# Layer norm shift as one float32r product of a rounded chunk, in a four-sub-layer hybrid decoder trunk on one core

## What is computed

```
def layer_norm(x, g, b):
    xf = x.astype(jnp.float32)
    mu = jnp.mean(xf, -1, keepdims=True)
    var = jnp.mean(jnp.square(xf - mu), -1, keepdims=True)
    return ((xf - mu) * lax.rsqrt(var + LN_EPS) * g + b).astype(x.dtype)

for i in range(DEPTH):                                   # DEPTH = 2, alpha = sqrt 2
    x = layer_norm(DN_ALPHA * x + 0.5 * swiglu(x, ...), ...)            # ln 0, 4
    y = swa_mixer(x, ...) if i == 0 else nsa_mixer(x, ...)
    x = layer_norm(DN_ALPHA * x + y, ...)                               # ln 1, 5
    x = layer_norm(DN_ALPHA * x + mem_cross_attention(x, mem, ...), ...) # ln 2, 6
    x = layer_norm(DN_ALPHA * x + 0.5 * swiglu(x, ...), ...)            # ln 3, 7
```

## Time and profile before

| | |
|---|---|
| Median of 3 runs | 2191.91 us (2190.52 to 2194.28) |
| Profiled execution | 2191.08 us, span 2189.3 us |
| PE busy | 2167.1 us, 99% |
| PEld busy | 1921.7 us, 88% |
| DVE, ACT, POOL busy | 1334.9 us (61%), 1063.5 us (49%), 780.2 us (36%) |
| Chain that ended last | PE 93%, DVE 3%, ACT 1%, POOL 1%, issue 1% |
| Mean granted clock of PE | 0.996 |

### The profile page before, as it was taken

The page is one execution under the profiler, slowest core; times in us unless marked ns, Lnnn a source line. Parts: engine busy times, 40 slices in busy tenths (PEclk is TensorE's granted clock), DMA queues, the critical chain, the costliest instruction groups (busy, mean ns, idle before and its releaser), DMA issues.

```text
span 2189.3 us, 35422 instructions
## 1 busy us (share of the span) xinstructions
PE 2167.1 (99%) x13654; PEld 1921.7 (88%) x13654; DVE 1334.9 (61%) x2315; ACT 1063.5 (49%) x1919; POOL 780.2 (36%) x573
## 2 busy tenths in 40 slices
PE   9999999999999999999999999999999999999998
PEld 8999998878888989898899999887778888989896
DVE  7666666464346938385756666657655346747475
ACT  5435345563445525254643444466654445535353
POOL 3201117557647030305420201555548555120203
PEclk9999999999999999999999999999999999999999
DMA  4333334213313323233232333320004312333332
GB/s 157 116 96 98 106 117 132 78 42 116 117 37 106 108 95 114 90 114 120 85 121 91 101 103 117 115 87 21 21 10 135 106 51 75 116 97 100 103 102 73
DMA packets 58199, 207.50 MB, mean 95 GB/s; under 512 B 6960, under 2 KB 7088, under 8 KB 57264
## 3 DMA queue, kind: packets, MB, share of 16 engines
q1 hardware_dynamic: 56016, 197.68, 29.0%
q10 hardware_dynamic: 2016, 7.55, 0.9%
HBM read 203.10 MB, written 2.10 MB: 94 GB/s over the span
## 4 chain that ended last, share of the span: by engine, by line
PE 93%; DVE 3%; ACT 1%; POOL 1%; issue 1%; DMA 0%; DVEq 0%; ACTq 0%
PE bank L1748 15%; PE bank L1749 14%; PE bank L1750 14%; PE bank L1959 11%; PE bank L1961 11%; PE bank L1960 11%; PE bank L2157 2%; PE bank L2118 2%; PE bank L2090 1%; PE bank L2091 1%; PE bank L1848 1%; PE bank L1849 1%; PE bank L1850 1%; PE bank L1767 1%; PE bank L1778 1%
## 5 line engine op out<-in xcount | busy, mean ns | idle before, releaser
L612 POOL TENSOR_TENSOR w_lo<-w_raw,w_hi 128x1024 fp32r<-128x1024 f32 (+1 forms) x226 | 530.4, 2355 | 1179.2 <-ACT w_hi L789 1179.1
L1748 PE MATMUL bank<-h_hi,w_hi 128*128 128x512 f32 x960 | 381.0, 397 | 2.5 <-DVE h_lo L1552 1.1
L1749 PE MATMUL bank<-h_lo,w_hi 128*128 128x512 f32 x960 | 374.4, 390 | 0.0
L1750 PE MATMUL bank<-h_hi,w_lo 128*128 128x512 f32 x960 | 374.0, 390 | 0.0
L789 ACT ACTIVATE w_hi<-w_raw 128x1024 fp32r<-128x1024 f32 (+1 forms) x227 | 230.5, 1021 | 128.3 <-PE bank L1750 92.4
L1959 PE MATMUL bank<-x_hi,w_hi 128*128 128x256 f32 x864 | 245.2, 284 | 0.3
L1960 PE MATMUL bank<-x_lo,w_hi 128*128 128x256 f32 x864 | 244.5, 283 | 0.0
L1961 PE MATMUL bank<-x_hi,w_lo 128*128 128x256 f32 x864 | 244.5, 283 | 0.0
L1748 PEld LDWEIGHTS bank<-h_hi,w_hi 128*128 128x128 f32 x960 | 180.4, 188 | 47.6 <-issue 4.7
L1750 PEld LDWEIGHTS bank<-h_hi,w_lo 128*128 128x128 f32 x960 | 180.2, 188 | 38.5
L1749 PEld LDWEIGHTS bank<-h_lo,w_hi 128*128 128x128 f32 x960 | 180.5, 188 | 36.1 <-issue 1.9
(11 more groups left out here) (306 smaller groups left out, 5708.1 us busy)
## 6 DMA issues: line engine op xcount, KB each, us to landing
w_raw<-w_dram SPq DMA_DIRECT2D x315, 512.0 KB, 3.5
w_raw<-w_dram SPq DMA_DIRECT2D x64, 448.0 KB, 3.3
f<-mem_dram ACTq DMA_DIRECT2D x5, 1024.0 KB, 6.5
out_dram<-t SPq DMA_DIRECT2D x8, 256.0 KB, 2.2
t<-x_dram SPq DMA_DIRECT2D x2, 512.0 KB, 6.7
f<-cmp_w_dram ACTq DMA_DIRECT2D x1, 1024.0 KB, 5.0
t<-x_dram ACTq DMA_DIRECT2D x2, 256.0 KB, 5.4
t<-x_dram ACTq DMA_DIRECT2D x1, 512.0 KB, 8.0
```

Of the source, the lines that this page charges most:

```text
L612: pool.tensor_tensor(w_lo[:, slot(s), 0:n * P], w_raw[:, s % RAW, 0:n * P], w_hi[:, slot(s), 0:n * P].bitcast(F32), ALU.subtract).then_inc ...
L1748: pe.matmul(dst, w_hi[:, slot(s), w], m_hi[:, k, :], start=k == 0, stop=False)
L1749: pe.matmul(dst, w_hi[:, slot(s), w], m_lo[:, k, :], start=False, stop=False)
L1750: last = pe.matmul(dst, w_lo[:, slot(s), w], m_hi[:, k, :], start=False, stop=k == n - 1)
```

## The change

Four edits:

1. `ones8`, the matrix of 8/1024, becomes float32r. It is still set once by POOL.
2. ACT gets a new instruction in each of the eight sub-layers, `lead_round`: it waits until DVE has added slab 0 to chunk 0 of `t`, and copies that chunk, rounded to float32r, to `lead` (the first part of the tile `pt`). `shift` waits for that copy and multiplies it instead of `t`.
3. `shift` stands behind out slab 2 instead of slab 1 where the sub-layer is no feed-forward (ln 1, 2, 5, 6).
4. `warm(8)` behind the statistics becomes `warm(5)`.

```
-        ones8 = sb("ones8", [P, P])
+        ones8 = sb("ones8", [P, P], F32R)
...
                     for j in range(KC):
                         feed(st.out[part][j] + 3)
+                        if not after and j == 0:
+                            lead_round(st)
...
+            def lead_round(st):
+
+                act.wait_ge(out_free, out_reads(st, len(st.out) - 1, 0))
+                act.activation(lead, t[:, 0, :], ACT.Copy).then_inc(lead_ready, 1)
...
             def out_squares(st, load=None):
                 for j in range(KC):
+                    if j == 0:
+                        lead_round(st)
                     feed(st.out[0][j] + 3)
                     square_chunk(st, j)
...
                 if not st.fill and st is not final:
-                    warm(8)
+                    warm(5)
...
             def shift(st):
                 pe.wait_ge(pool_set, 6)
-                pe.wait_ge(out_free, out_reads(st, len(st.out) - 1, 0))
-                pe.matmul(bank[B_SHIFT][:], ones8[:], t[:, 0, :], start=True, stop=True).then_inc(shift_ready, 1)
+                pe.wait_ge(lead_ready, st.ln + 1)
+                pe.matmul(bank[B_SHIFT][:], ones8[:], lead, start=True, stop=True).then_inc(shift_ready, 1)
...
-                    if j == 1 and part == len(st.out) - 1:
+                    if j == (1 if st.kind == "ffn" else 2) and part == len(st.out) - 1:
                         shift(st)
```

More of the change, by code:

```diff
@@ L365, in build @@
         t4 = [ptf[:, 1024 * i:1024 * i + 1024].rearrange("p (k s) -> p k s", k=4) for i in range(2)]
+        lead = pt[:, 0, :]
         comb = {1: (x_hi[:, 0:4, half[1]], x_lo[:, 0:4, half[1]]), 2: (rows4[0], rows4[1]), 3: (rows4[2], rows4[3]),
@@ L419, in build @@
         out_free = sem("out_free")
+        lead_ready = sem("lead_ready")
         shift_ready = sem("shift_ready")
@@ L616, in _ @@
             pool.memset(ones[:], 1.0 / D).then_inc(pool_set, 1)
-            pool.memset(ones8[:], 8.0 / D).then_inc(pool_set, 1)
+            pool.memset(ones8[:].bitcast(F32), 8.0 / D).then_inc(pool_set, 1)
             pool.memset(one, 1.0).then_inc(pool_set, 1)
```

## The result

| | before | after |
|---|---|---|
| Median | 2191.96 us (2190.52 to 2194.28, 22 runs) | 2195.31 us (2192.86 to 2198.81, 22 runs) |
| Ratio | | 1.0015, 95% interval 1.0009 to 1.0021 |
| Profiled execution | 2191.08 us, span 2189.3 us | 2197.56 us, span 2195.7 us |
| Mean granted clock | 0.996 | 0.993 |

The changed kernel is 3.35 us slower; 2194.8 us were predicted. 0.15% lies under the 0.2% that count as a change here, so it is no change by the stated bound, though the interval says that the small loss is real.

The account below looks back on a forecast made before the run. PE, busy 99% of the span, was taken to bound the kernel. Mixer stops +5.0, cheaper product -3.9, fewer ones -0.3 and clock +2.1 gave +2.9 us, 2194.8 us against the median; range 2190.5 to 2198.5.

Parts of the forecast that it names:

- The bound: Whole kernel: time is what PE's queue takes; an edit elsewhere counts only where it makes PE wait.
- The product: Shift at ln 0, 2, 3, 4, 6, 7: one float32r unit of 0.23 us, saving 0.65 us each, 3.9 together.
- The stops in the mixers: ln 1 and 5: copy ahead of rounding delays slab 3 by 2.5 us each, 5.0 together; PE stands still 3.2 us.
- its cheaper price: POOL's remainder of slab 3 in the mixers: 2.37 us alone, 2.69 beside DVE's sum of two squares.
- Slab 4 in the mixers: ln 1 and 5: two bases (2.54 us) and remainder done at 515.4 to 515.8, wanted at 516.0; no wait.
- a sign that POOL is tighter than it was put: Waits of PE at slab 4 in cross attention or mixers would show this; no size given.
- Fewer ones: ln 6: PE soon waits for POOL's first `x_lo`, so at most 0.35 us saved; 0.3 taken.
- The clock: Behind each mixer stop: falls in about 7 of 10 times, 3.4 us at half rate, 1.4 us each; 2.1 taken.
- the clock takes more: Rival, mixers: two stretches at half rate per stop, up to 3.1 us each, 6.2 together; total +7.0, 2198.9 us; chance 0.17.
- The sum: Whole kernel: +0.8 without the clock and +2.1 for it, +2.9 us, 2194.8 us against the median.
- The parts without the clock: Whole kernel: +5.0 for the mixers, -3.9 for the product, -0.3 for fewer ones, together +0.8 us.
- waits of up to 1.5 us leave no mark on the clock: PE's short waits in the trace, cited for the rival that stops come but the clock stays up: 2192.7 us, chance 0.16.

Follow-up runs that it names:

- the kernel with half the ones: The changed kernel with 6 products of ones instead of 12 in each mixer's stop, between shift and slab 3: median 2193.74 us, ratio 1.0006 of before.
- the kernel that rounds first: The changed kernel with ACT rounding slab 3 ahead of the copy in mixers and cross attention: 2185.05 us against 2191.82 before, ratio 0.9974.

## Why the prediction was right

**The bound.** PE's queue set the time throughout; each edit showed its worth in PE's starts. Right.

**The product.** 0.65 us each at six places. The new shift takes 0.22 us from its start to the next one, and the kernel with the product in the feed-forward alone has a span 2.6 us shorter, 4 x 0.65. In cross attention POOL's remainder was predicted to come with hardly any slack and no wait; that is what the rows show. Right.

**The stops in the mixers.** The path was right: the copy, the rounding behind it, POOL, slab 3. The chain behind DVE's addition was put at 4.16 us and was 4.19 in ln 1 and 4.20 in ln 5 (1654.45 - 1650.25). POOL's remainder took its cheaper price, 2.35 and 2.36 us: it escaped DVE's sum of two squares, which came at 512.39, behind it. So slab 3 is 2.4 us late in each mixer, not the 2.5 I took, and PE stands still for 2.9 us, not 3.2.

**Slab 4 in the mixers.** Here the prediction was wrong, and the falling clock hid it. It had two bases at 2.54 us and slab 4 without a wait, and named a wait there as a sign that POOL is tighter than it was put. But the bases meet the end of one sum on DVE (L1300, until 511.88) and the sum of two squares at 512.39, and take 3.41 us. In the changed kernel PE works slab 3 at half rate behind five of the six stops and needs 6.9 to 8.4 us for it, so POOL is in time. Behind the sixth, where the clock stayed up, slab 4 starts 5.78 us behind slab 3 instead of 5.46. So it does in both mixers with 12 and with 6 products of ones in the stop, and with the copy alone in the kernel before (5.77). That is 0.3 us, and slab 5 comes another 0.1 us late (5.52 to 5.57 us behind slab 4 instead of 5.44). So a mixer costs 2.8 us without the clock, two of them 5.7 against the 5.0 in the sum.

**Fewer ones.** 0.35 us, the bound that POOL's first `x_lo` set; 0.3 was taken. Right.

**The clock.** The mechanism was right and its size too small. I took a fall in 7 of 10 stops and 3.4 us at half rate, 2.1 us in all. Seen were five falls in six, two of them twice as long. Counting only the time at half rate in which PE had work, the three executions of the changed kernel lose 3.0 + 1.5, 1.7 + 3.0 and 1.7 + 0 us, on average 3.6. Each fall spares PE the 0.4 us by which slabs 4 and 5 are late otherwise, so 2.9 of that are net (an estimate from these rows). The kernels with and without ones in the stop differ by 3.3 us in the medians and by 2.6 in the ratios, and the two intervals together are wide enough to hold 2.1 too. That falls can be twice as long is what the rows show for certain. The rival "the clock takes more" was therefore half true: its mechanism, two stretches behind one stop, happened once in each of two executions and never at both stops of one, and it asked for 6.2 us in all.

**The sum.** The parts without the clock were put at +0.8 and came out at +0.2 by the medians and +0.7 by the ratio (1.0003, interval -1.3 to +2.6 us); the clock was put at +2.1 and came out at +2.6 to +3.3. That the total, +2.9 against +3.35, fits so well is in part luck: with the late slabs the rows themselves add up to some +1.6 us without the clock (5.7, less 3.9 and 0.35, and 0.1 us lost behind slab 4 in each cross attention), which is more than was measured. The kernel with the product in the feed-forward alone and the one with fewer ones also came out under the sums made from one profile, by 0.9 and 0.6 us by the ratio. Why is open; every one of them is inside its interval.

**The profiled execution** of the changed kernel was 6.4 us longer in span than that of before, not 3.35. It had 4.5 us of clock loss at the stops and one fall at 480 us, away from any of the moved instructions, which the two later executions don't have.

## What to carry to other kernels

A wait put into an in-order engine's program is paid by what stands behind it: look at what that engine does next and who needs it, here a weight rounding whose result had 0.9 us in hand came 3.2 us later behind a copy that waits for DVE. One swap of two calls turned a loss of 3.4 us into a gain of 6.8 (3.3 and 5.7 by the ratios). If TensorE must wait for some microseconds in a kernel that it bounds, count the stop, then the half rate behind it, and then the next thing that the same engines are late with: here the half rate hid that POOL was late for slab 4. If the stop can't be removed, products that compute nothing can be cheaper in it than none, as they were here.

## What was not expected of the hardware

- The clock came back only after 6.8 us in five of the nine falls at stops of 2.2 or 2.9 us, and after 3.4 in four, although PE worked without a pause from its first product of slab 3 on. The traces show what goes with it: in the five long ones the clock had fallen 0.7 to 1.0 us ahead of that first product (0.9 in the rows above, 510.55 against 511.46), in the four short ones 0.4 us ahead of it, at the same moment, or 1.2 and 1.3 us behind it. Here is a short one, the first mixer in the second profiled execution of the changed kernel, where slab 3 starts at 509.78 and the clock falls at 510.98:

```profile
510.00:511.00 1.00, 1.00 (x5) 0.80 (x5) 1.00 (x3) 0.98 (x2) 1.00 (x1) 0.99 0.47 53
511.00:514.00 3.00, 3.00 (x8) 2.32 (x7) 2.96 (x5) 2.66 (x4) 3.00 (x3) 0.50 0.40 157
514.00:515.00 1.00, 1.00 (x5) 0.82 (x4) 0.41 (x1) 0.13 (x1) 1.00 (x1) 0.81 0.00 0
```

The moment of the fall differs between executions of one kernel (510.55 - 508.55 = 2.0 us and 510.98 - 506.86 = 4.1 us behind the end of the shift), and no run sets it, so this is a reading of nine cases and not a cause shown.
- A standstill in two parts of 0.9 and 1.6 us with a float32 product of 0.88 us and three others between them left no fall at either mixer in the one profile taken; 0.9 and 2.2 us with a float32r product of 0.22 us between them brought one in four of four.
- The clock also falls at places that no edit touches, near 480 us, near 1462 to 1466 us in the second mixer, and at ln 6, in some executions of a kernel and not in others (480.06 in the kernel with half the ones, none there in the second and third of the changed one). The one in the second mixer comes 1.0 us (1461.8 in the kernel that rounds first) and 0.8 us (1466.3 with the copy alone in the kernel before) behind a wait of 1.5 us that every kernel here has. So the remark in the prediction that waits of up to 1.5 us leave no mark on the clock holds for the trace it was read from, and not for every execution. One such fall is worth up to 1.7 us, a part of the 3 to 6 us by which runs of one kernel differ.
